# The head norm of a first attention block on Trainium2: totals, reciprocals and roots moved from 8-partition rows to token layout

## The chip, the cores and the metric

The kernel runs on one core of one Trainium2 chip. The metric is the device time of one execution in microseconds. The time of a kernel is the median of its runs.

## The reference

Two blocks of layers in sequence (the first with a differential and a neighbourhood attention, the second with a hybrid mixer and experts), in float32, over 512 tokens and 256 context tokens with a model width of 1024. The change lies in the first block's first attention, a differential attention with 8 heads of width 128:

```python
def _diff_attend(q, k, v, lam, subln, lam_init):
    s = jnp.einsum('bqhjd,bkhjd->bhjqk', q, k).astype(jnp.float32) * (HEAD_DIM ** -0.5)
    p = jax.nn.softmax(s, axis=-1)
    a = (p[:, :, 0] - lam * p[:, :, 1]).astype(v.dtype)
    o = jnp.einsum('bhqk,bkhe->bqhe', a, v)
    o = rmsnorm(o, subln) * (1.0 - lam_init)
    return o.reshape(o.shape[0], o.shape[1], -1)
```

So each of the 768 tokens has, for each of the 8 heads, a root mean square over the head's 128 features, by which the head's output is divided. The result is multiplied by `wo` and added to the residual stream.

## The kernel before, in words

The program is a sequence of stages; each is one block in which the five engines run their own instruction lists, written out by hand, and wait for each other by semaphores. No scheduler reorders anything. Activations are kept with features on the 128 partitions and tokens along the free dimension, so the attention output `o` is a tile of 128 partitions x 8 heads x 768 tokens: one head per chunk of 768 columns. `differential` (from L1539) fills it, and also leaves `rs`, the sums of the exponentials, with tokens on the partitions: 128 x 6 token tiles x 8 heads. It doesn't divide by those sums; the norm's small term `eps` is scaled by their square instead.

`residual` (L1147) is the stage that follows. It multiplies the normed `o` by `wo` in fp32 split into a rounded high part and a low part. For this first attention it has a `Heads` object (L1071), the head norm, whose steps stand ahead of the product:

- `squares` (ACT, L1087): for each head, the squares of its 768 columns into one of two buffers. The third and later squares wait until the totals of the head two before have been taken (`summed`).
- `tensor` (PE): first six transposes (L1100) turn `rs` into rows, 8 partitions x 768 tokens. Then for each head n the totals over the 128 partitions (L1105): the weights are 8 columns of the constant `pick`, of which only column n is ones, the 768 squares stream, and the result accumulates in PSUM into row n of 8. Then five products that nobody reads (L1109, `HEADS_IDLE`). Then, when the roots have come, the spreads.
- `vector` (DVE): copies the turned sums (L1127), squares them times eps (L1129), adds the totals (L1132), takes the reciprocal (L1134), waits for ACT's root, rounds it (L1136, `root_hi`, in the order's rows `lo_4389`) and takes the low part (L276, `root_lo`, `lo_4390`). All of these are 8 partitions x 768.
- `roots` (ACT, L1091): the square root. In ACT's list it stands behind the rounding of two weight chunks (L791), and its first use loads ACT's table.
- `spread` (PE, L1119 and L1120): copies one row of the roots to all 128 partitions. There are two PSUM places: `res_acc`'s last slot and `res_totals`. Spread c waits from c = 2 on for the scaling of head c - 2.
- `scale` (DVE, L1143), `high` (ACT, L1095) and the low part (DVE, L276): one head's output is scaled, rounded and split.
- `ring.multiply` (L270, L271, L824 and later L263 to L265): the first two of the eight output chunks are computed head by head as these become ready, with the spread of head c + 2 ahead of the products of head c. The other six follow, densely.

Elsewhere the kernel has sums of squares in another form: `Squares.tensor` (L506) loads the 128x128 squares of a token tile as weights and streams one column of ones, so that the total comes out with tokens on the partitions. `unread_products` (L460) issues products of the identity with constants that nobody reads. The same helper's lines are used in several stages.

Of the kernel before, what the change touches and what calls it, by code (L numbers as in the profile page):

```python
# [20 lines left out]
ACT = mybir.ActivationFunctionType  # L21
F32 = mybir.dt.float32
# [5 lines left out]
P = 128  # L28
D = 1024
KD = D // P  # L30
# [155 lines left out]
class Core:  # L186
# [5 lines left out]
    def __init__(self, nc):  # L192
        self.nc, self.n, self.fresh, self.spent, self.place = nc, 0, [], [], {}
        self.n_zeroing = 2 * (NE + NOVER)
# [79 lines left out]
def lo_of(engine, lo, value, hi):  # L274

    return engine.tensor_tensor(lo, value, hi.bitcast(F32), ALU.subtract)  # L276
# [180 lines left out]
def unread_products(K, bank, count):  # L457

    for _ in range(count):
        K.nc.tensor.matmul(bank, K.const("ident"), K.consts[:, 0:bank.shape[1]], start=True, stop=True)  # L460


class Squares:
# [37 lines left out]
    def tensor(self, pe):  # L501
        nc, one = self.K.nc, self.K.const("ones")[:, 0:1]

        def total(at, tile, tokens):
            for t in range(tokens // P):
                last = nc.tensor.matmul(self.totals[:, at + t:at + t + 1], tile[:, t * P:(t + 1) * P], one, start=True, stop=True)  # L506
            return last

        final = self.room[(KD - 1) % 2]
        pe.wait_ge(self.summed, KD - 2)  # L510
        last = total(0, self.sums, self.tok + self.extra)
        if self.weight is not None:
            last = total(NT, self.weighed, self.tok)
        last.then_inc(self.early, 1)
        if self.idle is not None:
            unread_products(self.K, self.totals[:, 640:896], 2)
        pe.wait_ge(self.squared, KD)
        last = total(512, final[0], self.tok)
        if self.weight is not None:
            last = total(512 + NT, final[1], self.tok)  # L520
        last.then_inc(self.late, 1)
        if self.idle is not None:
            unread_products(self.K, self.idle, 1)

    def vector(self, dve):
        nc, totals, ms, inv = self.K.nc, self.totals, self.ms, self.inv
        n, own = (self.tok + self.extra) // P, self.tok // P
        dve.wait_ge(self.early, 1)
        nc.vector.tensor_scalar(ms[:, 0:n], totals[:, 0:n], 1.0 / D, EPS, ALU.mult, ALU.add)
        if self.weight is not None:  # L530
            nc.vector.tensor_scalar(ms[:, NT:], totals[:, NT:NT + NTX], 1.0 / D, None, ALU.mult)
        dve.drain()
        dve.wait_ge(self.late, 1)
        nc.vector.scalar_tensor_tensor(ms[:, 0:own], totals[:, 512:512 + own], 1.0 / D, ms[:, 0:own], ALU.mult, ALU.add)
        if self.weight is not None:
            nc.vector.scalar_tensor_tensor(ms[:, NT:], totals[:, 512 + NT:512 + NT + NTX], 1.0 / D, ms[:, NT:], ALU.mult, ALU.add)
        dve.drain()
        last = nc.vector.reciprocal(inv[:, 0:n], ms[:, 0:n])
        if self.weight is not None:
            dve.drain()  # L540
            nc.vector.tensor_tensor(ms[:, NT:], ms[:, NT:], inv[:, 0:NTX], ALU.mult)
            dve.drain()
            nc.vector.tensor_scalar(ms[:, NT:], ms[:, NT:], EPS, None, ALU.add)
            dve.drain()
            last = nc.vector.reciprocal(inv[:, NT:], ms[:, NT:])
        last.then_inc(self.inverted, 1)
        if self.weight is not None:
            roots = self.K.roots
            dve.wait_ge(self.rooted, 1)
            nc.vector.tensor_tensor(roots[:, NT + NTX:], roots[:, 0:NTX], roots[:, NT:NT + NTX], ALU.mult)  # L550
            dve.drain()
# [207 lines left out]


ACCS = 3
HEADS_IDLE = 5


class Ring:
# [305 lines left out]
class Heads:  # L1071


    def __init__(self, K, ctx, src, tok, sums, eps, gain, room, totals, spreads, idle):
        self.K, self.src, self.tok, self.sums, self.eps, self.gain = K, src, tok, sums, eps, gain
        self.room, self.totals, self.spreads, self.idle = room, totals, spreads, idle
        self.rstd, self.floor = (K.sb(ctx, "heads_" + n, [KD, tok]) for n in ("rstd", "floor"))
        self.root_hi, self.root_lo = K.lo(self.floor), K.lo(self.rstd)
        self.rows = K.sb(ctx, "heads_rows", [KD, KD], FR)
        self.floor_full, self.squared, self.summed, self.inverted, self.rooted, self.split, self.spread_full, self.scaled, self.rounded = (  # L1080
            K.sem("heads_" + n) for n in ("floor", "squared", "summed", "inverted", "rooted", "split", "spread", "scaled", "hi"))

    def squares(self, act):
        for n in range(KD):
# [3 lines left out]

    def roots(self, act):
        act.wait_ge(self.inverted, 1)  # L1090
        self.K.nc.scalar.activation(self.rstd[:], self.rstd[:], ACT.Sqrt).then_inc(self.rooted, 1)  # L1091

    def high(self, act, hi, c):
        act.wait_ge(self.scaled, c + 1)
        self.K.nc.scalar.copy(hi[:, c, :], self.src[:, c, 0:self.tok]).then_inc(self.rounded, 1)  # L1095

    def tensor(self, pe, parts):
        nc, pick, ident = self.K.nc, self.K.const("pick"), self.K.const("ident")
        for t in range(self.tok // P):
            last = nc.tensor.transpose(self.spreads[0][0:KD, t * P:(t + 1) * P], self.sums[:, t, :], ident)  # L1100
        last.then_inc(self.floor_full, 1)
        for n in range(KD):
            pe.wait_ge(self.squared, n + 1)
            for a, b in parts:
                last = nc.tensor.matmul(self.totals[0:KD, a:b], pick[:, KD - 1 - n:2 * KD - 1 - n], self.room[n % 2][0][:, a:b],  # L1105
                                        start=(n == 0), stop=(n == KD - 1))
            last.then_inc(self.summed, 1)
        for _ in range(HEADS_IDLE):
            nc.tensor.matmul(self.idle, ident, self.K.consts[:, 0:512], start=True, stop=True)  # L1109
        pe.wait_ge(self.split, 1)  # L1110
        for c in range(2):
            self.spread(pe, c, parts)
# [8 lines left out]
        last.then_inc(self.spread_full, 1)  # L1121

    def vector(self, dve):
        nc, tok, rstd, floor = self.K.nc, self.tok, self.rstd, self.floor
        nc.vector.tensor_copy(self.rows[:], self.K.const("ident")[0:KD, 0:KD])
        dve.wait_ge(self.floor_full, 1)
        nc.vector.tensor_copy(rstd[:], self.spreads[0][0:KD, 0:tok])  # L1127
        dve.drain()
        nc.vector.scalar_tensor_tensor(floor[:], rstd[:], self.eps, rstd[:], ALU.mult, ALU.mult)  # L1129
        dve.drain()  # L1130
        dve.wait_ge(self.summed, KD)
        nc.vector.scalar_tensor_tensor(rstd[:], self.totals[0:KD, 0:tok], 1.0 / P, floor[:], ALU.mult, ALU.add)  # L1132
        dve.drain()
        nc.vector.reciprocal(rstd[:], rstd[:]).then_inc(self.inverted, 1)  # L1134
        dve.wait_ge(self.rooted, 1)
        nc.vector.tensor_copy(self.root_hi[:], rstd[:])  # L1136
        dve.drain()
        lo_of(nc.vector, self.root_lo[:], rstd[:], self.root_hi[:]).then_inc(self.split, 1)

    def scale(self, dve, c):  # L1140
        mine = self.src[:, c, 0:self.tok]
# [2933 lines left out]
```

## Time and profile before

| | us |
|---|---|
| median of 3 runs | 3480.74 |
| the runs | 3481.81, 3480.74, 3475.3 |
| the profiled execution | 3483.02 |
| its span | 3481.2 |
| PE busy | 3284.4 |
| DVE busy | 2272.3 |
| ACT busy | 1477.7 |
| POOL busy | 340.8 |

The median is of executions without a profile. The span is from the first to the last instruction of the profiled one; what is beyond it up to 3483.02 us lies before and after. The page shows by slices of 87 us how busy each engine is, and the clock that TensorE was granted, which has two levels, 2.4 GHz (1.00) and 1.2 GHz (0.50). PE is the engine for matmuls and PEld its weight loads, DVE is VectorE, ACT is ScalarE, POOL is GpSimd and SP is SyncE. One fp32 matmul shows as two records. Times in the trace are counted from the start of the span. The changed stage takes less than 30 us of it, so the slices are too coarse for it, and the trace is read by stretches and by instructions.

### The profile page before, as it was taken

How to read it: one execution, taken by the hardware profiler on the slowest of the kernel's cores; microseconds unless marked ns; L12 is line 12 of the kernel's file. 1: busy time of each engine (PE TensorE's matmuls, PEld its weight loads, DVE VectorE, ACT ScalarE, POOL GpSimd, SP SyncE). 2: the span in 40 equal slices, each digit the busy share in tenths (PEclk: the TensorE clock that was granted, in tenths of full speed). 3: DMA queues.
4: the chain of work that ended last, by engine and by line, in shares of the span. 5: the costliest groups of instructions: out<-in, count | busy, mean ns of one | idle time of the engine just before them, and what ended most of it. 6: DMA issues, size and time to landing. Idle time of an engine off the chain costs nothing. (4 is left out here: it accounts for less than half of the span.)

```text
span 3481.2 us, 46855 instructions
## 1 busy us (share of the span) xinstructions
PE 3284.4 (94%) x18748; PEld 2682.1 (77%) x18748; DVE 2272.3 (65%) x2962; ACT 1477.7 (42%) x1957; POOL 340.8 (10%) x217
## 2 busy tenths in 40 slices
PE   7998999999999999999999998899889989999996
PEld 5886778888888896778888778779677766777774
DVE  6467746756666227758776555665765358888885
ACT  5216633212123117733233443443433247777774
POOL 0020000000000000000000013321200013222221
PEclk9999999999999999999999999999999999999998
DMA  6540013354533221045654239111023259999993
GB/s 246 197 167 13 1 49 109 115 175 134 177 109 100 71 72 44 22 131 189 225 182 130 74 92 273 30 37 49 25 61 85 61 207 380 384 369 366 380 359 114
DMA packets 371666, 522.63 MB, mean 150 GB/s; under 512 B 19618, under 2 KB 313122, under 8 KB 345872
## 3 DMA queue, kind: packets, MB, share of 16 engines
q1 hardware_dynamic: 362112, 503.25, 43.1%
q0 software_dynamic: 9360, 16.72, 1.4%
q8 instruction: 129, 2.11, 0.2%
q14 instruction: 65, 0.53, 0.0%
HBM read 484.46 MB, written 51.90 MB: 154 GB/s over the span
## 5 line engine op out<-in xcount | busy, mean ns | idle before, releaser
L276 DVE TENSOR_TENSOR lo<-exp_raw,exp_hi 128x2048 fp32r<-128x2048 f32 x192 | 439.0, 2290 | 65.1 <-ACT exp_hi L3651 65.1
L3651 ACT CAST exp_hi<-exp_raw 128x2048 fp32r<-128x2048 f32 x192 | 366.5, 1913 | 113.4 <-PE exp_down_acc L265 49.6
L264 PE MATMUL ffn_acc<-lo,up_w_hi 128*128 128x512 f32 x1140 | 406.7, 357 | 0.0
L263 PE MATMUL ffn_acc<-normed_hi,up_w_hi 128*128 128x512 f32 x1008 | 360.0, 357 | 11.0 <-DVE lo L276 11.0
L444 DVE SCALAR_TENSOR_TENSOR aside_w<-aside_w,aside_c 128x1024 f32<-128x1024 f32 x176 | 213.0, 1233 | 81.2 <-DMA aside_w<-in_ada_t 73.0
L264 PEld LDWEIGHTS ffn_acc<-lo,up_w_hi 128*128 128x128 f32 x1140 | 216.0, 189 | 33.5
L263 PEld LDWEIGHTS ffn_acc<-normed_hi,up_w_hi 128*128 128x128 f32 x1008 | 190.8, 189 | 41.7 <-DVE lo L276 12.6
L1418 ACT ACTIVATE conv<-ffn_acc,vecs 128x768 f32<-128x768 f32 (+1 forms) x88 | 73.1, 881 | 297.7 <-PE ffn_acc L265 297.7
L265 PE MATMUL ffn_acc<-normed_hi,lo 128*128 128x512 f32 (+1 forms) x528 | 190.0, 360 | 0.0
L265 PE MATMUL ffn_acc<-gated_hi,lo 128*128 128x512 f32 (+1 forms) x528 | 187.9, 356 | 0.0
L265 PE MATMUL ffn_acc<-normed_hi,up_w_lo 128*128 128x512 f32 x480 | 170.4, 355 | 0.0
L1483 DVE SCALAR_TENSOR_TENSOR conv<-ffn_acc,vecs,conv 128x511 f32<-128x511 f32 (+1 forms) x132 | 79.1, 655 | 125.0 <-ACT conv L1418 125.0
L263 PE MATMUL ffn_acc<-gated_hi,down_w_hi 128*128 128x512 f32 (+1 forms) x396 | 142.1, 359 | 3.6 <-DVE lo L276 3.6
L264 PE MATMUL ffn_acc<-lo,down_w_hi 128*128 128x512 f32 (+1 forms) x396 | 142.2, 359 | 0.0
L265 PE MATMUL feat_acc<-normed_hi,lo 128*128 128x512 f32 (+1 forms) x400 | 139.0, 348 | 0.0
L263 PE MATMUL feat_acc<-normed_hi,lo 128*128 128x512 f32 x368 | 127.3, 346 | 1.6 <-DVEq L728 1.6
L264 PE MATMUL feat_acc<-lo,lo 128*128 128x512 f32 x368 | 127.6, 347 | 0.0
L263 PE MATMUL tok_acc<-tok_w_hi,normed_hi 128*128 128x256 f32 x384 | 114.2, 297 | 3.0 <-DVEq L1039 1.7
L276 POOL TENSOR_TENSOR lo<-res_w,res_w_hi 128x1024 fp32r<-128x1024 f32 x4 | 9.6, 2419 | 1062.2 <-ACT res_w_hi L685 1062.2
L265 PEld LDWEIGHTS ffn_acc<-normed_hi,lo 128*128 128x128 f32 x528 | 100.4, 190 | 15.0
L265 PEld LDWEIGHTS ffn_acc<-gated_hi,lo 128*128 128x128 f32 x528 | 100.1, 190 | 15.0
L264 PE MATMUL tok_acc<-lo,normed_hi 128*128 128x256 f32 x384 | 107.3, 279 | 0.0
(677 smaller groups left out, 8920.6 us busy)
## 6 DMA issues: line engine op xcount, KB each, us to landing
exp_raw<-in_w_experts SPq DMA_DIRECT2D x192, 1024.0 KB, 8.2
aside_w<-in_ada_t SPq DMA_DIRECT2D x176, 512.0 KB, 6.3
up_w<-in_ffn_up SPq DMA_DIRECT2D x88, 512.0 KB, 5.2
x_rows<-dn_zero SPq DMA_DIRECT2D x42, 384.0 KB, 5.3
y_rows<-dn_zero SPq DMA_DIRECT2D x42, 384.0 KB, 5.3
ada_w<-in_ada_first SPq DMA_DIRECT2D x8, 1024.0 KB, 13.0
v<-in_ada_t SPq DMA_DIRECT2D x16, 512.0 KB, 6.7
gate_w<-in_w_in SPq DMA_DIRECT2D x16, 512.0 KB, 5.3
```

The costliest lines, as they stand in the source:

```text
L263: nc.tensor.matmul(out, left[0], right[0], start=start, stop=False)
L264: nc.tensor.matmul(out, left[0], right[1], start=False, stop=False)
L265: return nc.tensor.matmul(out, left[1], right[0], start=False, stop=stop)
L276: return engine.tensor_tensor(lo, value, hi.bitcast(F32), ALU.subtract)
L444: self.K.nc.vector.scalar_tensor_tensor(tile[:], tile[:], 1.0, self.cond[layer // 2, s][:], ALU.mult, ALU.mult, accum_out=self.K.mods[:, l ...
L1418: last = nc.scalar.activation(conv[:, u, s, :], acc[:, u, s, 0:tok], ACT.Identity, bias=K.vecs[:, at(n + (b0 + n0 + s * NF))], scale=K.vec ...
L1483: nc.vector.scalar_tensor_tensor(conv[:, u, s, a + 1:b], acc[:, u, s, a:b - 1], K.vecs[:, at(n + (tap0 + n0 + s * NF))], conv[:, u, s, a + ...
L3651: nc.scalar.copy(hi[slot(e, j)][:], raw[tile(e, j)][:]).then_inc(tile_hi[j], 1)
```

## The change

Everything up to the roots stays with tokens on the partitions. The totals are taken with the squares of a token tile as weights and one column of ones streaming, 48 products in all (8 heads x 6 tiles), each with its own column of PSUM. The sums `rs` are used as they lie. DVE's square, addition and reciprocal, and ACT's root, work on 128 partitions x 48. PE then turns the roots into 8 rows x 768 by six transposes; DVE rounds and splits them straight from PSUM. The five unread products become one behind the totals and one behind the transposes.

```diff
@@ -759,7 +759,6 @@
 
 
 ACCS = 3
-HEADS_IDLE = 5
 
 
 class Ring:
@@ -1077,8 +1076,9 @@
         self.rstd, self.floor = (K.sb(ctx, "heads_" + n, [KD, tok]) for n in ("rstd", "floor"))
         self.root_hi, self.root_lo = K.lo(self.floor), K.lo(self.rstd)
         self.rows = K.sb(ctx, "heads_rows", [KD, KD], FR)
-        self.floor_full, self.squared, self.summed, self.inverted, self.rooted, self.split, self.spread_full, self.scaled, self.rounded = (
-            K.sem("heads_" + n) for n in ("floor", "squared", "summed", "inverted", "rooted", "split", "spread", "scaled", "hi"))
+        self.floors, self.inverse, self.turnable = (K.sb(ctx, "heads_" + n, [P, tok // P, KD]) for n in ("floors", "inverse", "roots"))
+        self.turned, self.squared, self.summed, self.inverted, self.rooted, self.split, self.spread_full, self.scaled, self.rounded = (
+            K.sem("heads_" + n) for n in ("turned", "squared", "summed", "inverted", "rooted", "split", "spread", "scaled", "hi"))
 
     def squares(self, act):
         for n in range(KD):
@@ -1088,25 +1088,27 @@
 
     def roots(self, act):
         act.wait_ge(self.inverted, 1)
-        self.K.nc.scalar.activation(self.rstd[:], self.rstd[:], ACT.Sqrt).then_inc(self.rooted, 1)
+        self.K.nc.scalar.activation(self.turnable[:], self.inverse[:], ACT.Sqrt).then_inc(self.rooted, 1)
 
     def high(self, act, hi, c):
         act.wait_ge(self.scaled, c + 1)
         self.K.nc.scalar.copy(hi[:, c, :], self.src[:, c, 0:self.tok]).then_inc(self.rounded, 1)
 
     def tensor(self, pe, parts):
-        nc, pick, ident = self.K.nc, self.K.const("pick"), self.K.const("ident")
-        for t in range(self.tok // P):
-            last = nc.tensor.transpose(self.spreads[0][0:KD, t * P:(t + 1) * P], self.sums[:, t, :], ident)
-        last.then_inc(self.floor_full, 1)
+        nc, one, ident = self.K.nc, self.K.const("ones")[:, 0:1], self.K.const("ident")
+        tiles = self.tok // P
         for n in range(KD):
             pe.wait_ge(self.squared, n + 1)
-            for a, b in parts:
-                last = nc.tensor.matmul(self.totals[0:KD, a:b], pick[:, KD - 1 - n:2 * KD - 1 - n], self.room[n % 2][0][:, a:b],
-                                        start=(n == 0), stop=(n == KD - 1))
+            for t in range(tiles):
+                last = nc.tensor.matmul(self.totals[:, t * KD + n:t * KD + n + 1], self.room[n % 2][0][:, t * P:(t + 1) * P], one,
+                                        start=True, stop=True)
             last.then_inc(self.summed, 1)
-        for _ in range(HEADS_IDLE):
-            nc.tensor.matmul(self.idle, ident, self.K.consts[:, 0:512], start=True, stop=True)
+        unread_products(self.K, self.idle, 1)
+        pe.wait_ge(self.rooted, 1)
+        for t in range(tiles):
+            last = nc.tensor.transpose(self.spreads[0][0:KD, t * P:(t + 1) * P], self.turnable[:, t, :], ident)
+        last.then_inc(self.turned, 1)
+        unread_products(self.K, self.idle, 1)
         pe.wait_ge(self.split, 1)
         for c in range(2):
             self.spread(pe, c, parts)
@@ -1121,21 +1123,20 @@
         last.then_inc(self.spread_full, 1)
 
     def vector(self, dve):
-        nc, tok, rstd, floor = self.K.nc, self.tok, self.rstd, self.floor
+        nc, tok = self.K.nc, self.tok
         nc.vector.tensor_copy(self.rows[:], self.K.const("ident")[0:KD, 0:KD])
-        dve.wait_ge(self.floor_full, 1)
-        nc.vector.tensor_copy(rstd[:], self.spreads[0][0:KD, 0:tok])
-        dve.drain()
-        nc.vector.scalar_tensor_tensor(floor[:], rstd[:], self.eps, rstd[:], ALU.mult, ALU.mult)
+        nc.vector.scalar_tensor_tensor(self.floors[:], self.sums, self.eps, self.sums, ALU.mult, ALU.mult)
         dve.drain()
         dve.wait_ge(self.summed, KD)
-        nc.vector.scalar_tensor_tensor(rstd[:], self.totals[0:KD, 0:tok], 1.0 / P, floor[:], ALU.mult, ALU.add)
+        nc.vector.scalar_tensor_tensor(self.floors[:], self.totals[:, 0:tok // P * KD].rearrange("p (t n) -> p t n", n=KD), 1.0 / P,
+                                       self.floors[:], ALU.mult, ALU.add)
         dve.drain()
-        nc.vector.reciprocal(rstd[:], rstd[:]).then_inc(self.inverted, 1)
-        dve.wait_ge(self.rooted, 1)
-        nc.vector.tensor_copy(self.root_hi[:], rstd[:])
+        nc.vector.reciprocal(self.inverse[:], self.floors[:]).then_inc(self.inverted, 1)
+        dve.wait_ge(self.turned, 1)
+        turned = self.spreads[0][0:KD, 0:tok]
+        nc.vector.tensor_copy(self.root_hi[:], turned)
         dve.drain()
-        lo_of(nc.vector, self.root_lo[:], rstd[:], self.root_hi[:]).then_inc(self.split, 1)
+        nc.vector.tensor_tensor(self.root_lo[:], turned, self.root_hi[:].bitcast(F32), ALU.subtract).then_inc(self.split, 1)
 
     def scale(self, dve, c):
         mine = self.src[:, c, 0:self.tok]
```

On PE, in the stage of the head norm, from its start to the first spread. Names: `square_216` and `square_217` are the two buffers, `rs` the sums, `res_acc` and `res_totals` PSUM. Before:

```order
L1100 MATMUL res_acc<-consts,rs 8x128 x6
L1105 MATMUL res_totals<-square_216,consts 8x512
L1105 MATMUL res_totals<-square_216,consts 8x256
L1105 MATMUL res_totals<-square_217,consts 8x512
L1105 MATMUL res_totals<-square_217,consts 8x256
...
L1109 MATMUL res_acc<-consts 128x512 x5
L1119 MATMUL res_acc<-lo_4389,heads_rows 128x512
L1120 MATMUL res_acc<-lo_4390,heads_rows 128x512
```

And now:

```order
L1103 MATMUL res_totals<-consts,square_216 128x1 x6
L1103 MATMUL res_totals<-consts,square_217 128x1 x6
...
L460 MATMUL res_acc<-consts 128x512
L1109 MATMUL res_acc<-consts,heads_roots 8x128 x6
L460 MATMUL res_acc<-consts 128x512
L1121 MATMUL res_acc<-lo_4389,heads_rows 128x512
L1122 MATMUL res_acc<-lo_4390,heads_rows 128x512
```

The sixteen streaming products (of 512 and 256 columns) became eight groups of six products of one column; the transposes moved from ahead of them to behind them; three of the five unread products are gone.

On DVE, in the same place. Before:

```order
L1125 CAST heads_rows<-consts 8x8
L1127 COPY heads_rstd<-res_acc 8x768
L1129 SCALAR_TENSOR_TENSOR heads_floor<-heads_rstd 8x768
L1132 SCALAR_TENSOR_TENSOR heads_rstd<-res_totals,heads_floor 8x768
L1134 RECIPROCAL heads_rstd<-heads_rstd 8x768
L1136 CAST lo_4389<-heads_rstd 8x768
L276 TENSOR_TENSOR lo_4390<-heads_rstd,lo_4389 8x768
L1143 SCALAR_TENSOR_TENSOR o<-o,subln,res_acc 128x768
```

And now:

```order
L1127 CAST heads_rows<-consts 8x8
L1128 SCALAR_TENSOR_TENSOR heads_floors<-rs 128x48
L1131 SCALAR_TENSOR_TENSOR heads_floors<-res_totals,heads_floors 128x48
L1134 RECIPROCAL heads_inverse<-heads_floors 128x48
L1137 CAST lo_4389<-res_acc 8x768
L1139 TENSOR_TENSOR lo_4390<-res_acc,lo_4389 8x768
L1144 SCALAR_TENSOR_TENSOR o<-o,subln,res_acc 128x768
```

One copy is gone, three operations shrank from 8 x 768 to 128 x 48, and the last two now read PSUM.

## Rows read from the trace of the kernel before

**Rows 1.** The page, part 1: busy time, share of span, instructions.

```profile
PE 3284.4 (94%) x18748; PEld 2682.1 (77%) x18748; DVE 2272.3 (65%) x2962; ACT 1477.7 (42%) x1957; POOL 340.8 (10%) x217
```

**Rows 2.** Stretches: length, busy us (instructions) per engine, granted clock, DMA share, GB/s.

```profile
432.00:434.00 2.00, 1.12 (x8) 0.69 (x7) 0.00 (x0) 0.75 (x3) 0.00 (x0) 1.00 0.00 0
...
450.20:454.20 4.00, 0.01 (x1) 0.00 (x0) 3.02 (x3) 0.84 (x1) 0.00 (x0) 0.76 0.00 0
454.20:462.30 8.10, 8.05 (x23) 6.59 (x24) 4.69 (x5) 2.50 (x3) 0.00 (x0) 0.50 0.01 2
462.30:482.50 20.20, 20.20 (x106) 16.12 (x105) 12.72 (x14) 4.18 (x5) 0.00 (x0) 1.00 0.00 0
```

**Rows 3.** Timeline of the head norm: start, length, engine, line [idle before, releaser].

```profile
434.36 0.82 PE L1100 MATMUL res_acc<-consts,rs 128*8 128x128 f32 x6 [0.61 <-PEq L250]
435.24 10.49 PE L1105 MATMUL res_totals<-square,consts 128*8 128x512 f32 x32
438.02 0.84 ACT L1087 ACTIVATE square<-o 128x768 f32<-128x768 f32 x1 [0.45 <-PE res_totals L1105]
443.93 1.98 ACT L791 CAST lo<-v 128x1024 fp32r<-128x1024 f32 x2
445.65 4.56 PE L1109 MATMUL res_acc<-consts 128*128 128x512 f32 x10
445.76 0.95 DVE L1132 SCALAR_TENSOR_TENSOR heads_rstd<-res_totals,heads_floor 8x768 f32<-8x768 f32 x1 [8.57 <-PE res_totals L1105]
445.92 1.28 ACT L1091 ACT_TABLE_LOAD   x1
446.78 4.94 DVE L1134 RECIPROCAL heads_rstd<-heads_rstd 8x768 f32<-8x768 f32 x1
451.76 0.84 ACT L1091 ACTIVATE heads_rstd<-heads_rstd 8x768 f32<-8x768 f32 x1 [4.55 <-DVE heads_rstd L1134]
452.63 0.55 DVE L1136 CAST lo<-heads_rstd 8x768 fp32r<-8x768 f32 x1 [0.91 <-ACT heads_rstd L1091]
453.25 0.95 DVE L276 TENSOR_TENSOR lo<-heads_rstd,lo 8x768 fp32r<-8x768 f32 x1
454.25 0.79 PE L1119 MATMUL res_acc<-lo,heads_rows 8*128 8x512 f32 x1 [4.04 <-DVE lo L276]
```

**Rows 4.** Timeline, PE: first product of the third, fourth and fifth spread.

```profile
457.00 0.79 PE L1119 MATMUL res_acc<-lo,heads_rows 8*128 8x512 f32 x1
...
462.64 0.49 PE L1119 MATMUL res_totals<-lo,heads_rows 8*128 8x512 f32 x1
...
465.80 0.50 PE L1119 MATMUL res_acc<-lo,heads_rows 8*128 8x512 f32 x1
```

**Rows 5.** Timeline, PE, end of the same stage: one-column totals at clock 1.00.

```profile
532.48 1.40 PE L506 MATMUL res_totals<-consts,square_sums 128*128 128x1 f32 x12
533.74 1.11 PE L460 MATMUL res_totals<-consts 128*128 128x256 f32 x4
```

**Rows 6.** Timeline, PE, start of the program: one-column totals.

```profile
14.12 2.72 PE L506 MATMUL ada_totals<-consts,square_sums 128*128 128x1 f32 x12 [14.12 <-DMA rows<-in_rows]
16.71 2.70 PE L506 MATMUL ada_totals<-consts,square 128*128 128x1 f32 x12
```

**Rows 7.** Stretches at the end of the second feed-forward stage.

```profile
1909.70:1913.10 3.40, 3.40 (x29) 3.30 (x28) 0.56 (x5) 2.52 (x3) 0.00 (x0) 1.00 0.00 0
1913.10:1916.50 3.40, 3.10 (x9) 1.56 (x9) 1.27 (x9) 0.21 (x1) 0.00 (x0) 0.51 0.00 0
```

**Rows 8.** Timeline, PE, there.

```profile
1908.78 1.39 PE L506 MATMUL ffn_acc<-consts,square_sums 128*128 128x1 f32 x12
1910.03 1.03 PE L506 MATMUL ffn_acc<-consts,weighed_sums 128*128 128x1 f32 x8
1910.93 1.11 PE L460 MATMUL ffn_acc<-consts 128*128 128x256 f32 x4
1911.87 2.25 PE L506 MATMUL ffn_acc<-consts,conv 128*128 128x1 f32 x16
```

**Rows 9.** Lines L538 and L556: durations in ns, min/median/max.

```profile
L538 DVE RECIPROCAL inverse<-mean_squares x6: 178/192/193, 19.7 to 2821.0; 128x6 f32<-128x6 f32 x4, 128x4 f32<-128x4 f32 x2
...
L556 ACT ACTIVATE roots<-inverse x6: 205/208/212, 22.3 to 2821.2; 128x6 f32<-128x6 f32 x3, 128x4 f32<-128x4 f32 x2, 128x10 f32<-128x10 f32 x1
```

## The prediction

> **What bounds the kernel now.** I read the page's first table first: PE is busy for 3284.4 us, 94% of the span [rows 1]. A change to a small stage therefore counts by what it does to the stretches in which PE waits and by the speed at which PE runs. The chain that ended last shows only the end of the program, so I read the stage itself: first by stretches [rows 2], then in order of time [rows 3]. The head norm begins at 434.3 us and ends, for this question, where the first matmul of the spread starts, at 454.25. What the reader should see in it:
>
> - 435.24 to 445.7: the eight totals. PE is busy without a gap. The 32 records take 10.49 us, 1.3 a head, of which ACT's square is 0.84; before each square ACT waits 0.45 for PE (six such rows). PE sets this pace.
> - 445.76 to 454.25: a serial chain of 8.5 us. DVE adds the floor (0.95), takes reciprocals on 8 partitions x 768 (4.94), ACT takes roots (0.84), DVE rounds (0.55) and takes the low part (0.95). PE fills the first 4.5 us with unread products and then idles for 4.0.
> - After that idle stretch the granted clock is 0.50 for 8.1 us and returns to 1.00 at about 462.3 [rows 2].
>
> The price of the low clock in the part that follows: one head's spread and products take 3.16 us at full clock (462.64 to 465.80), while those that began at 457.00 took 5.64 [rows 4]. Had the clock been full from 454.25 on, the third spread after the first (462.64) would have come at about 459.6: spread 0.9, scaling 1.0, rounding 0.85 and products 2.3 (3.16 less the spread) in sequence, with 0.3 of hops. So the low clock costs 3.0 us there.
>
> **The totals.** The number of PE cycles doesn't change. Before, 8 columns of `pick` are the weights and 768 squares stream past. Now the squares are the weights, in six loads of 128x128, and one column of ones streams. The stage that sums squares at 532.48 shows this form: six products, twelve records, take 1.26 us from start to start of what follows [rows 5]. Eight heads are 10.1 to 10.3 us, against 10.5. So at full clock the totals gain 0.2 to 0.4 us, no more. The six transposes of the sums and two DVE passes that vanish from the start were hidden behind ACT's first square and the totals: nothing.
>
> **The clock during the totals** is the term that decides. The same products ran at the start of the program for over 5 us in one piece, twelve records in 2.59 us and twice as long as the 1.26 above, so at 1.2 GHz, and the second twelve were no faster than the first [rows 6]. And from 1909.70 to 1913.10 PE shows 3.40 us busy of 3.40 at clock 1.00, and the next stretch is at 0.51 [rows 7]. What PE did before that fall was almost nothing but such one-column products: 36 records from 1908.78 on, with one pair of unread products between them [rows 8]. The fall came 4.3 us after their start. In the changed kernel they run for over 10 us with nothing else in between. I therefore take the clock to fall to 1.2 GHz within the totals. The Trainium skill says otherwise: TensorE: Matmul & The Clock Gate, Part 1, has the clock gate follow how busy PE has been and warns of idle gaps; by it a queue without gaps stays at full clock, and the sum would end at -7.1 us (the rival below). By that rule, the trace disagrees: PE was busy for all 3.40 us ahead of the fall [rows 7].
>
> When does it fall? Between 435.2 (at once) and 440 (4.3 us in, and a little more). In the case at 1909 PE came from dense products; here it comes from the thin end of the attention, busy for 1.12 us of 2 [rows 2]. I take 437. Then 1.4 heads run at 1.28 us and 6.6 at 2.56 (twelve records at the start of the program took 2.59 [rows 6]): 1.8 + 16.9, so the totals end at 453.9 instead of 445.7. With the bounds: 455.7 and 451.0.
>
> **From the last total to the first spread.** Now the arithmetic is 128 x 48. Adding the floor: 0.2 us, as the smallest DVE operations. Reciprocal: 0.19 us for six columns [rows 9] and 4.94 for 768 [rows 3] give 6.2 ns a column, so 0.45. With the gaps of the engine, inverted after 0.75. Root: 0.26 (0.21 for six columns [rows 9]). The loading of ACT's table takes 1.28 us and stands behind two roundings of 1.98 [rows 3]; at the slow pace the last square ends 4.3 us before the totals do, so both are over in time and cost nothing. Without that cover, at full clock, they end 3.3 us after the last square, 1.65 after the last total, and hold the root back by 0.9. Next PE: the one unread product behind the totals takes 0.9 us at full clock (five in 4.56 us [rows 3]) and 1.8 at half, so PE is ready at 1.8, after the root. Here the change adds a wait: PE stands for ACT's root, and behind it in PE's list are the transposes and all spreads, for which DVE and ACT's eight roundings wait. Six transposes: 0.82 us at full clock [rows 3], 1.5 at half: 3.3. DVE then rounds and subtracts straight from PSUM. The trace has no such rounding; the nearest rows are 0.55 for the rounding from SBUF and 0.95 for an operation of the same size that reads PSUM (445.76), and I take the latter, since the source is what changes: 0.95 + 0.07 + 0.95. The second unread product runs beside it. Sum 5.4 us, against 8.5 before. So the first spread starts at 459.3, not 454.25: **+5.05 us** (bounds +2.2 and +6.9, from the fall at 440 and at 435.2).
>
> **The clock after it.** Before, the low clock lasted 8 us beyond the first spread and cost 3.0. Now PE has been at work on two unread products, the transposes and the spreads from 453.9 on, with short waits, so it should come back sooner; 8.1 us after the work began, as here with its waits, would be 462, and it can be sooner. What can be won is between 0 and 3.0; I take 1.2, below the middle, since the waits stay between.
>
> Sum: +5.05 - 1.2 = **+3.9 us**. The profiled execution took 3483.02 us for its span of 3481.2, so 3486.9; it stood 2.3 us above the median of 3480.74, which gives **3484.6**. The bounds are -0.8 and +6.9, with the runs shown spread over 6.5 us besides.
>
> Nothing else moves. The DMA loads of the stage land at its start. All of this is small: about 0.2%, or 7 us, is what a measurement of this kernel can tell from no change.
>
> **Rivals.**
> - *Slower: the clock falls at once and stays low through two more heads.* For it: the attention's end is thin and the six transposes that ran at 434.36 are gone [rows 3]; low stretches after waits lasted 8 us already. Against it: two unread products. Price: totals to 455.7, spread at 461.1 (+6.9), and the low clock up to two us longer than before beyond the spread, +1 to +2: about +8.5, 3489. It decides if the fall comes before 436 and the return after 464. 0.18.
> - *Faster: the clock holds.* Totals end at 445.4; the root waits for ACT's table; spread 4.8 us later, at 450.2, -4.05; with no 4 us of idleness the clock stays up and the 3.0 are won too: -7.1, 3473.7. Against it stand [rows 6] and [rows 7]; for it, only that PE has no gap. 0.12.
> - *The clock holds in the totals and falls after them*, as before: only -4, 3476.7. 0.04.
> - *The chain is not much shorter*, if DVE's three operations on 128x48 cost nearer the 0.95 of the old form than 0.2 to 0.45: about 2 us more, 3486.7. The 0.19 us for six columns speaks against it. 0.02.
>
> **How the numbers follow.** My forecast has 0.64: between -0.8 and +6.9, with the likeliest value at 3484.6. The range of 3477 to 3491 takes in its bounds, the slow rival and some of the spread between runs; what is left out is the clock that holds and part of the tails. Faster by over 0.2% (below 3473.8): half of the clock that holds, 0.07 with a stray run. Slower by over 0.2% (above 3487.7): most of the slow rival and the upper end of the forecast, 0.22. Within: 0.71.
>
> **What would show it.** In the profile of the changed kernel: a granted clock of 0.50 before 440 and through most of the totals; the 96 one-column records, twelve in about 2.6 us; DVE's 128x48 reciprocal under 0.6 us; the table load finished before the reciprocal ends; the first spread near 459; full clock again by 463. If instead twelve of them take 1.3 us throughout, the deciding step is wrong and the kernel is faster by about 7 us. If the first spread comes near 459 but the time is unchanged, the return of the clock was worth the full 3 us.

## The result, and the profile after

Over 22 runs of each, the changed kernel takes 3485.78 us (median) against 3479.71 us: a ratio of 1.0015, with a 95% interval of 1.001 to 1.0021. It is slower by 6.1 us between the medians, or by 5 us as the ratio has it (0.15% of 3480): clear of noise, and inside the 0.2% that the prediction named as its bound. The forecast was 3484.6 us; it expected +3.9 us, and +6.1 came.

The profiled execution took 3490.07 us, the slowest of its 22, so its trace shows an expensive case. The page:

```profile
span 3488.1 us, 46969 instructions
PE 3293.1 (94%) x18806; PEld 2696.3 (77%) x18806; DVE 2264.9 (65%) x2961; ACT 1477.5 (42%) x1957; POOL 339.7 (10%) x217
```

The stage by stretches, the changed kernel (columns as in [rows 2]): the last 2 us before and in the first totals, the totals, the chain to the first spread, the head-by-head part; three pieces around the clock's return at 459.6, its fall at 463.0 and its next return at 480.1 (0.50 in between); and all that follows.

```profile
434.30:436.30 2.00, 0.82 (x5) 0.82 (x5) 0.27 (x2) 1.58 (x2) 0.00 (x0) 0.85 0.22 46
...
435.48:455.90 20.42, 20.42 (x97) 20.42 (x97) 0.00 (x0) 8.90 (x10) 0.00 (x0) 0.51 0.20 52
455.90:461.18 5.28, 4.39 (x12) 1.66 (x11) 2.55 (x4) 0.24 (x1) 0.00 (x0) 0.65 0.00 0
461.18:493.90 32.72, 32.31 (x128) 25.58 (x129) 17.45 (x19) 6.67 (x8) 0.00 (x0) 0.74 0.00 1
...
459.60:463.00 3.40, 2.34 (x10) 1.26 (x8) 2.27 (x3) 0.00 (x0) 0.00 (x0) 1.00 0.00 0
463.00:466.40 3.40, 3.15 (x9) 2.53 (x10) 3.40 (x5) 2.06 (x3) 0.00 (x0) 0.50 0.00 0
...
480.10:484.00 3.90, 3.90 (x20) 2.96 (x19) 1.88 (x2) 0.83 (x1) 0.00 (x0) 1.00 0.00 0
...
493.90:3488.10 2994.20, 2842.91 (x16022) 2321.36 (x16020) 1956.64 (x2478) 1265.11 (x1539) 308.83 (x195) 0.98 0.47 156
```

In the kernel before, the same three pieces of the stage are:

```profile
435.24:445.70 10.46, 10.46 (x33) 2.81 (x33) 1.87 (x2) 7.41 (x9) 0.00 (x0) 1.00 0.37 100
445.70:454.25 8.55, 4.51 (x11) 1.77 (x10) 7.38 (x4) 2.33 (x3) 0.00 (x0) 0.88 0.00 0
454.25:482.57 28.32, 28.32 (x129) 22.77 (x129) 17.48 (x19) 6.67 (x8) 0.00 (x0) 0.85 0.00 1
...
482.57:3481.20 2998.63, 2847.74 (x16022) 2327.08 (x16020) 1958.13 (x2478) 1265.04 (x1539) 309.40 (x195) 0.98 0.47 156
```

The totals grew from 10.5 us to 20.4, the chain shrank from 8.55 to 5.28, and the head-by-head part grew from 28.3 to 32.7. The stage ends 11.3 us later (493.90 against 482.57). The rest of the program, whose code is the same, happened to be 4.4 us shorter in this execution (2994.2 against 2998.6).

In order of time, the changed kernel, to be held against [rows 3]:

```profile
435.48 20.45 PE L1103 MATMUL res_totals<-consts,square 128*128 128x1 f32 x96 [1.48 <-ACT square L1087]
...
450.84 0.84 ACT L1087 ACTIVATE square<-o 128x768 f32<-128x768 f32 x1 [1.72 <-PE res_totals L1103]
...
453.58 1.28 ACT L1091 ACT_TABLE_LOAD   x1
455.79 2.06 PE L460 MATMUL res_acc<-consts 128*128 128x512 f32 x2
455.96 0.21 DVE L1131 SCALAR_TENSOR_TENSOR heads_floors<-res_totals,heads_floors 128x48 f32<-128x48 f32 x1 [21.09 <-PE res_totals L1103]
456.24 0.45 DVE L1134 RECIPROCAL heads_inverse<-heads_floors 128x48 f32<-128x48 f32 x1
456.73 0.24 ACT L1091 ACTIVATE heads_roots<-heads_inverse 128x48 f32<-128x48 f32 x1 [1.86 <-DVE heads_inverse L1134]
457.63 1.49 PE L1109 MATMUL res_acc<-consts,heads_roots 128*8 128x128 f32 x6
459.16 0.95 DVE L1137 CAST lo<-res_acc 8x768 fp32r<-8x768 f32 x1 [2.46 <-PE res_acc L1109]
460.18 0.94 DVE L1139 TENSOR_TENSOR lo<-res_acc,lo 8x768 fp32r<-8x768 f32 x1
461.18 0.49 PE L1121 MATMUL res_acc<-lo,heads_rows 8*128 8x512 f32 x1 [0.89 <-DVE lo L1139]
```

The reader should see three things. PE has no gap in the totals, and the clock is 0.50 all the same; ACT's idle time before each square rose from 0.45 to 1.72 us because it waits for PE. The reciprocal fell from 4.94 us to 0.45 and the root from 0.84 to 0.24. And the table load is over at 454.86 (453.58 and 1.28), before the reciprocal begins at 456.24, so the root never waits for it.

### The profile page after: what moved, and what is told of

Its sections match the earlier page's. It is cut to its first block and busy times, and to the rows that moved or that the text cites. A ratio compares the mean times of both kernels' runs of the same rounds, so it can differ in the third digit from the quotient of the medians.

```text
span 3488.1 us, 46969 instructions
## 1 busy us (share of the span) xinstructions
PE 3293.1 (94%) x18806; PEld 2696.3 (77%) x18806; DVE 2264.9 (65%) x2961; ACT 1477.5 (42%) x1957; POOL 339.7 (10%) x217
## 5 line engine op out<-in xcount | busy, mean ns | idle before, releaser
L263 PE MATMUL ffn_acc<-normed_hi,up_w_hi 128*128 128x512 f32 x1008 | 360.2, 357 | 10.8 <-DVE lo L276 10.8
L263 PEld LDWEIGHTS ffn_acc<-normed_hi,up_w_hi 128*128 128x128 f32 x1008 | 190.7, 189 | 41.9 <-DVE lo L276 12.4
L263 PE MATMUL ffn_acc<-gated_hi,down_w_hi 128*128 128x512 f32 (+1 forms) x396 | 140.9, 356 | 3.0 <-DVE lo L276 3.0
L263 PE MATMUL feat_acc<-normed_hi,lo 128*128 128x512 f32 x368 | 127.1, 345 | 1.6 <-DVEq L728 1.6
L263 PE MATMUL tok_acc<-tok_w_hi,normed_hi 128*128 128x256 f32 x384 | 114.7, 299 | 3.2 <-DVEq L1038 1.7
L265 PE MATMUL tok_acc<-tok_w_hi,lo 128*128 128x256 f32 x384 | 108.1, 281 | 0.0
```

Source lines behind the costliest of these rows:

```text
L263: nc.tensor.matmul(out, left[0], right[0], start=start, stop=False)
L265: return nc.tensor.matmul(out, left[1], right[0], start=False, stop=stop)
```

## The experiments

All of them concern this one stage. For each trace I read two lengths: from ACT's first square to the first spread, and from there to the first product of the dense part (L263). The ratio is against the kernel before, run on the same chip at the same time. Where the text gives us for a ratio, they are its share of 3480 us; the medians themselves give somewhat other values (e5 -2.0, e7 -8.4, e8 -14.3).

| kernel | to the first spread | to the dense part | ratio (95%) |
|---|---|---|---|
| before, two traces | 19.91, 19.91 | 28.3, 30.4 | 1 |
| changed, three traces | 26.6, 26.8, 26.8 | 32.7, 27.9, 27.9 | 1.0015 (1.001 to 1.0021) |
| e1, 128 columns in the totals | 17.9 | 26.8 | 0.9983 (0.9975 to 0.9992) |
| e2, changed with spreads of 128 partitions | 26.5 | 23.3 | 1.0006 (0.9997 to 1.0015) |
| e3, before with nine unread products | 19.9 | 25.2 | 0.9997 (0.9988 to 1.0006) |
| e4, row totals, arithmetic in token layout | 18.6 | 26.7 | 0.9982 (0.9973 to 0.999) |
| e5, e1 with the root earlier | 17.4 | 26.7 | 0.999 (0.998 to 1.0) |
| e6, e5 with spreads of 128 partitions | 17.5 | 23.3 | 0.9984 (0.9975 to 0.9993) |
| e7, e6 with an unread product at the start | 15.9 | 23.3 | 0.9974 (0.9962 to 0.9985) |
| e8, e4 with both | 17.1 | 23.3 | 0.9962 (0.9949 to 0.9976) |
| e9, before with spreads of 128 partitions | 19.9 | 24.3 | 0.9982 (0.9973 to 0.9991) |

One trace can't rank two of these kernels by its whole length. Behind the stage all of them run the same code, and that code took from 2989.5 us (e8) to 3004.1 us (e7) in these traces, a wider spread than any effect in the table. So the stage is read from the traces, and the time from the medians and ratios.

**e1: the same weight loads, more columns.** The totals' `one` becomes 128 columns of ones; the column of PSUM follows the order of issue, so that later products overwrite what isn't needed.

```diff
-                last = nc.tensor.matmul(self.totals[:, t * KD + n:t * KD + n + 1], self.room[n % 2][0][:, t * P:(t + 1) * P], one,
+                at = n * tiles + t
+                last = nc.tensor.matmul(self.totals[:, at:at + P], self.room[n % 2][0][:, t * P:(t + 1) * P], ones,
```

> The changed kernel, but each of the 48 totals streams 128 columns of ones instead of one; the further columns are overwritten or never read. Same weight loads, same number of products. Theory (the one-column products let the clock fall): the granted clock stays at 1.00 through the totals, a group of twelve records takes 1.3 to 1.45 us, the totals end near 446.5 instead of 455.8, the first spread comes at 451 to 452. Against the kernel before: -2 to -6 us, depending on whether the clock falls later in the short waits. Rival (the fall comes from the thin end of the attention, or from the waits at the stage's start, whatever the products are): the clock falls near 436 as before, a group takes 2.6 us or more, and the time is +6 us or worse.

```profile
434.50:437.80 3.30, 3.03 (x14) 3.03 (x15) 0.00 (x0) 1.01 (x3) 0.00 (x0) 0.50 0.89 248
437.80:447.00 9.20, 9.20 (x84) 9.20 (x84) 0.00 (x0) 6.62 (x8) 0.00 (x0) 1.00 0.11 27
447.00:451.75 4.75, 2.72 (x12) 0.96 (x11) 2.55 (x4) 1.79 (x3) 0.00 (x0) 1.00 0.00 0
451.75:478.51 26.76, 26.35 (x128) 21.20 (x129) 17.44 (x19) 6.68 (x8) 0.00 (x0) 0.94 0.00 1
```

This decides between the two explanations. PE was busy without a gap in both forms; only the number of streamed columns differs, and here the clock rose to 1.00 within the totals at 437.8 and stayed there, where with one column it stayed at 0.50 to the end. The first 3.3 us are low here too, which the expectation had not allowed for, so the start of the stage has a low stretch of its own (see e7). e5, e6 and e7 stream 128 columns as well, and in each of their traces the clock is at 1.00 for the last 9 us of the totals or more. The kernel is 0.17% faster than before, as expected, and 0.32% faster than the changed one by the two ratios.

**e2: spreads that read 128 partitions.** `rstd`, `floor` and `rows` get 128 partitions; DVE clears the first two at the start, and the roots still fill eight of them.

```diff
-        row = self.rows[:, c:c + 1].broadcast_to([KD, P])
+        row = self.rows[:, c:c + 1].broadcast_to([P, P])
...
+        zeros = self.K.x[:, 0, 0:tok]
+        nc.vector.tensor_tensor(self.root_hi[:], zeros, zeros, ALU.subtract)
+        nc.vector.tensor_tensor(self.root_lo[:], zeros, zeros, ALU.subtract)
```

> The changed kernel, but the spreads read all 128 partitions (zeros beyond the eight rows of roots) instead of 8; columns and count are the same, so PE's time for them at a given clock is the same. Theory (spreads from eight partitions don't bring the clock back, which is why it stayed low for 17 us beside a PE that had no gap): the totals still run at the low clock to about 455.8 and the first spread comes at about 461, but the clock is at 1.00 for good by 468 instead of 480.1, and the time is +2 to +4 us against before instead of +6. Rival (the number of partitions doesn't matter, the long low stretch comes from the waits): low until about 480 again, +6 us.

```profile
436.11:456.30 20.19, 20.19 (x96) 20.19 (x97) 1.14 (x4) 8.90 (x10) 0.00 (x0) 0.51 0.20 53
456.30:461.72 5.42, 4.62 (x12) 1.80 (x12) 2.55 (x4) 0.24 (x1) 0.00 (x0) 0.63 0.00 0
461.72:484.99 23.27, 22.86 (x128) 19.78 (x129) 17.44 (x19) 6.68 (x8) 0.00 (x0) 1.00 0.00 1
```

The totals are as low and as long as in the changed kernel, the second trace of one-column totals that shows this. The head-by-head part went from 27.9 or 32.7 us to 23.3 at clock 1.00. The measured 1.0006, some 3 us less than the changed kernel's, agrees with the expected +2 to +4 against before, though its interval reaches to no change and overlaps the changed kernel's.

**e3: PE's gap filled in the kernel before.** `HEADS_IDLE = 9` in place of 5.

> The kernel before, with nine unread products behind the totals instead of five, which fill PE's 4.0 us of idle time (5 products took 4.56 us, so 9 take some 7.8 of the 8.5). Theory (the low clock after that gap costs 3.0 us): clock 1.00 from 450 to 463 in most executions, -2 to -3 us against before. Rival (the clock falls in the part after the first spread anyway, because of its own waits): 0 to -1 us.

```profile
433.58:444.00 10.42, 10.42 (x32) 2.77 (x33) 1.88 (x2) 7.37 (x9) 0.00 (x0) 1.00 0.36 101
444.00:452.60 8.60, 7.99 (x19) 3.34 (x19) 7.38 (x4) 2.38 (x3) 0.00 (x0) 1.00 0.00 0
452.60:477.79 25.19, 24.78 (x129) 19.93 (x129) 17.45 (x19) 6.68 (x8) 0.00 (x0) 1.00 0.00 1
```

In the trace the clock never falls, and the head-by-head part takes 25.2 us instead of 28.3: the low clock had cost 3.1, where the prediction had 3.0. Yet the ratio is 0.9997 with 1 in its interval, so against -2 to -3 us expected the time shows -1 and can't be told from no change. The mechanism is seen in the trace; that it is worth anything in the median is not shown.

**e4: half of the change.** The totals go back to the form before, into rows; DVE copies them out, six transposes turn them, and the 128 x 48 arithmetic and the way back stay as changed.

```diff
+        nc.vector.tensor_copy(self.rstd[:], self.totals[0:KD, 0:tok]).then_inc(self.kept, 1)
...
+        pe.wait_ge(self.kept, 1)
+        for t in range(tiles):
+            at = BACK + t * KD
+            last = nc.tensor.transpose(self.spreads[0][:, at:at + KD], self.rstd[:, t * P:(t + 1) * P], ident[0:KD, 0:KD])
+        last.then_inc(self.back, 1)
```

> Half of the change alone: the totals as in the kernel before (768 columns stream past 8 columns of weights, result in eight rows), then copied out of PSUM and turned to token layout by six transposes; floor, reciprocal and root on 128 x 48 and the way back as in the changed kernel. Theory (the arithmetic in token layout is a gain, the loss is the clock in the totals): clock 1.00 through the totals, which end at 445.7; the first spread about 6.3 us later, at 452.0 against 454.25 before; -1 to -4 us against before. Rival (the shorter chain is eaten by the added copy, transposes and hops): the first spread at 454 or later, no gain.

```profile
435.40 12.18 PE L1105 MATMUL res_totals<-square,consts 128*8 128x512 f32 x32 [1.48 <-ACT square L1089]
...
448.62 0.53 PE L1112 MATMUL res_acc<-consts,heads_rstd 8*128 8x8 f32 x6
...
450.25 0.82 PE L1117 MATMUL res_acc<-consts,heads_roots 128*8 128x128 f32 x6
```

The chain after the totals takes 5.5 us, where 6.3 was expected. The totals took 12.2 us and not 10.5, because this form too has the low stretch at the start (the clock was 0.50 from 436.2 to 439.7), which I had not expected. Even so: 0.9982. The arithmetic in token layout is a gain; with either other form of totals, e1's or this one, the kernel is faster than before, and only with the one-column form is it slower.

**e5: the root ahead of ACT's weight roundings.** In ACT's list `heads.roots` moves before the two `ring.high`, and a second unread product follows the transposes.

> The kernel of e1 (128 columns stream in the totals), with ACT's root ahead of the rounding of two weight chunks, so that its table is loaded during the last totals, and a second unread product behind the transposes. Theory (the root waited for the table: 448.58 to 448.8 in e1, 0.7 us after the reciprocal): root 1.05 us after the last total, first spread 3.9 us after it instead of 4.5 to 4.7; -0.6 us against e1, and a little more where the added unread product keeps the clock: about -6.5 us against before. Rival (the roundings of the weights, now later, hold up the first rounding of a head): -5 us or less, with ACT busy with weights when the first head is scaled.

The first spread comes 4.0 us after the last total's end (447.0 to 450.98) instead of e1's 4.6, about as expected, and the trace's stage is 0.6 us shorter than e1's. The rival's cause isn't seen: ACT is done with the weights at 449.92 and then idle for 3.1 us before the first head's rounding. The time is 0.999, -3.5 us instead of -6.5, and the intervals of e1 and e5 overlap: a step of half a microsecond is below what these runs can tell.

**e6: e5 with the spreads of e2.**

> The kernel of e5 with spreads that read 128 partitions, as in e2. Theory (products from eight partitions don't hold the clock; that is why in e1 it fell at 454.9 for 3.4 us): clock 1.00 from the totals to the end of the head-by-head part in most executions, -7 to -9 us against before. Rival (the short waits between the spreads let it fall): as e5, -6 us.

The head-by-head part takes 23.3 us at clock 1.00, and the time is 0.9984, or -5.6 us; expected were -7 to -9.

**e7: e6 with one unread product at the start.**

```diff
+        unread_products(self.K, self.idle, 1)
         for n in range(KD):
             pe.wait_ge(self.squared, n + 1)
```

> The kernel of e6 with one more unread product at the start of the stage, in the 0.9 us in which PE waits for ACT's first square. Theory (the low clock from 434.4 to 437.8 in e1, and from 436.2 to 439.7 in e4, comes from that wait together with the thin end of the attention): no low clock at the start of the totals, which then take 11.3 us instead of 12.3; -1 us against e6, -8 to -10 against before. Rival (one product of 0.9 us is too little): as e6.

```profile
433.37 1.10 PE L460 MATMUL res_acc<-consts 128*128 128x512 f32 x2 [0.61 <-PEq L250]
434.30 10.93 PE L1105 MATMUL res_totals<-consts,square 128*128 128x128 f32 x96
```

The totals take 10.9 us instead of 12.4 or 12.6, with no low clock at their start. The three kernels whose list at the start held the transposes (before, e3, e9) didn't have it either; the six without them and without this product (changed, e1, e2, e4, e5, e6) all had it. The six transposes that the change moved away from there seem to have done a job that no one had given them; no run puts them back alone, but the split is complete. 0.9974, -9 us, where -8 to -10 was expected; its interval overlaps e6's.

**e8: e4 with the spreads of e2 and the unread product at the start.**

> The kernel of e4 (row totals, arithmetic in token layout) with spreads from 128 partitions and the unread product at the start. Theory: totals 10.5 us at full clock, the chain after them 5.5 us, no low clock in the stage; the first spread at about 451.5; -8 to -10 us against before, within 1 us of e7, whose totals are 0.8 us longer and whose chain is 1.6 us shorter. Rival (the clock falls in the chain's waits all the same): as e4, -6 us.

```profile
433.20:444.70 11.50, 11.46 (x35) 3.09 (x35) 2.02 (x4) 8.28 (x10) 0.00 (x0) 1.00 0.34 91
444.70:450.30 5.60, 4.36 (x19) 1.76 (x19) 3.50 (x5) 1.76 (x3) 0.00 (x0) 1.00 0.00 0
450.30:473.57 23.27, 22.86 (x128) 19.80 (x129) 17.46 (x19) 6.69 (x8) 0.00 (x0) 1.00 0.00 1
```

Clock 1.00 in the whole stage, and the lowest ratio of all: 0.9962, -13 us, faster than both kernels, from five runs. That it beats e7 is not shown: the intervals overlap, and e7's stage is 1.2 us the shorter in the traces (39.1 against 40.3). The stage itself is 7.9 us shorter than in the first trace of before. The interval begins at 0.9976, -8.4 us, so the trace's saving lies just short of it. The rest lies behind the stage in this trace: the same code took 2989.5 us there against 2998.6, and the granted clock over the whole execution was 0.983 against 0.978. Whether the edit brings that about or the executions happened so is not settled, and I wouldn't count on more than the 8 or 9.

**The changed kernel and the one before again.**

> The changed kernel again, for a second trace. Theory (one-column totals always let the clock fall; how long it stays low after the spreads depends on where its changes happen to lie against the stage): the totals again at 0.50 from before 440 to about 455.8, the clock back at 1.00 at some time between 459 and 480, and the first product of the dense part (493.9 in the first trace, 482.6 in the kernel before) between 485 and 494. Rival (the 17 us of low clock are fixed by the kernel): low until 480 again, 493.9.

> The changed kernel a third time, with the same expectations as for the second: if the three traces differ in when the clock comes back, but not in the totals, the theory holds.

> The kernel before again. Theory: totals at clock 1.00; after the gap of PE's 4.0 us the clock falls in some executions and in others perhaps later, and comes back at different times, so the dense part starts between 479.5 and 486 (482.6 in the first trace).

These are single executions, taken for their traces: 3487.08 and 3488.32 us for the changed kernel, 3484.0 for the one before.

The changed kernel, second trace:

```profile
434.20:454.50 20.30, 20.26 (x95) 20.26 (x96) 0.00 (x0) 8.94 (x10) 0.00 (x0) 0.50 0.19 52
...
458.10:461.50 3.40, 2.26 (x9) 1.23 (x9) 2.26 (x3) 0.00 (x0) 0.00 (x0) 1.00 0.00 0
461.50:468.30 6.80, 6.54 (x20) 4.90 (x19) 4.30 (x5) 2.50 (x3) 0.00 (x0) 0.50 0.00 0
468.30:488.00 19.70, 19.70 (x104) 15.92 (x104) 12.73 (x14) 4.18 (x5) 0.00 (x0) 1.00 0.00 1
```

The totals are the same in all three traces; what differs is how long the clock stays low afterwards: 17 us in the first, 6.8 in the other two. In the kernel before it was 10.3 and, in the second trace, 13.6 (453.3 to 466.9), with the dense part at 484.5. The rival of a fixed 17 us falls.

**e9: only the spreads changed, in the kernel before.**

> The kernel before, with only the spreads changed: they read 128 partitions (zeros beyond the eight rows). Theory (beside the clock, the change of the weights' partitions costs PE 0.2 us on either side of each spread, 0.4 us a head: 3.17 us in the kernel with nine unread products against 2.77 in e2): the first spread at the same 19.9 us after the first square as before; from there to the dense part 23.3 to 25.5 us instead of 28.3, with the clock falling at most for a window's worth after PE's gap; -2.5 to -5 us against before, ratio 0.9986 to 0.9993. Rival (the gain in e2, e6, e7 and e8 came from their other edits): 28 us again, ratio 1.000.

```profile
444.40:453.01 8.61, 4.57 (x12) 1.82 (x11) 7.38 (x4) 2.39 (x3) 0.00 (x0) 1.00 0.00 0
453.01:477.35 24.34, 24.07 (x129) 20.79 (x130) 17.46 (x19) 6.69 (x8) 0.00 (x0) 0.93 0.00 1
```

24.3 us, within the 23.3 to 25.5 expected, and 0.9982, slightly more of a gain than expected. The clock did fall after PE's 4 us gap, at 454.4, but was back by 457.8. The gain of the full spreads stands on its own.

## Why the prediction was right, and where it was off

- **"The number of PE cycles doesn't change."** Right as far as the runs show: no trace has the one-column totals at full clock, but their 20.45 us at half clock would be 10.2 at full, against 10.49 before. e7, with 128 columns at full clock, takes 10.9.
- **"The clock during the totals."** Right, and the deciding step. It was at 0.50 in all four traces with one-column totals, beside a busy PE. The rule that a queue without gaps holds the clock, from the Trainium skill (TensorE: Matmul & The Clock Gate, Part 1), would have given -7. By that rule, the traces disagree: e1 and the changed kernel differ in the totals only in the columns, PE shows no gap in either, and the clock is 1.00 in one from 437.8 on and 0.50 in the other to the end.
- **"When does it fall?"** This is the first mis-sized term. I took 437, between 435.2 and 440; in the first trace it came at 435.7, 0.2 us behind the first total's start, and in the two others at 434.2 and 434.3, just before it. I had the thin end of the attention in view, but costed the removed transposes at nothing; e7 shows that PE's idle 0.9 us in their place is part of the cause. So the totals took all of the 20.4 us, and the first spread came 6.7 to 6.9 us later than before instead of 5.05: the upper bound that I had worked out.
- **"From the last total to the first spread," 5.4 us.** 5.39 (455.79 to 461.18), with the parts as priced: 0.21 and 0.45 on DVE (0.2, 0.45), 0.24 for the root (0.26), 1.49 for the transposes (1.5), 0.95 and 0.94 from PSUM (0.95 each), the table load hidden. At full clock, too: I had 4.8 with the wait for the table, and e1 has 4.7.
- **"The clock after it," -1.2 us.** The second mis-sized term, and the wrong step in kind. The clock did come back early, at 459.6, before the first spread; then it fell again at 463.0, after a wait for DVE and two spreads. From the first spread to the dense part the three traces take 32.7, 27.9 and 27.9 us, 29.5 on average, and the two of before 28.3 and 30.4, 29.3. The credit was nothing. 5.05 and -1.2 became 6.8 and 0.2, a sum of 7 from few traces, where the median says 6.1. Both errors point the same way. That the time still fell within 1.2 us of the forecast is in part luck: the sum was 2.2 us short, but it stood on 3480.74 us for the kernel before, and the median of all its runs is 3479.71.
- **The slower rival**, which I gave 0.18, is what the traces show: it was to decide if the clock fell before 436 and returned after 464. It fell before 436 in all three, and came back for good at 480.1 in the first and at 468 in the other two (with 3.4 us of full clock in between, which it did not foresee). Its price of +8.5 was too high for the median, which is between it and the forecast.
- **The faster rivals** are out: the totals ran at half clock each time. So is the chain that is not much shorter: DVE's three operations on 128x48 took 0.19, 0.21 and 0.45 us.
- **A misread row.** I counted six rows in which ACT waits 0.45 for PE before a square. There are five; the sixth wait, the first of them, is 0.81. Nothing in the sum hangs on it.

## What to carry to other kernels

Moving an arithmetic chain from 8 partitions to 128 shortens it as its rows say (here 8.5 us to 5.3), but the form of the products that go with it has to be judged as well, not for their cycles but for the clock that they leave behind: here 20 us of one-column products ran at 1.2 GHz in all four traces, however busy PE looked. If such a form is wanted for its layout, let it stream more columns, whose results may be overwritten (128 were enough here), or keep the old form and turn its result. And before costing a removed instruction at nothing, look at what the engine's clock does around it: the six transposes here were priced at nothing, and only where they stood, or an unread product in their place, were the totals free of a low stretch of 3.4 us at the start.

## What the runs showed that I had not expected

**The partitions of the weights cost PE time.** In the head-by-head part at clock 1.00 throughout, 25.2 us with spreads from 8 partitions (e3) became 23.3 with 128 (e2, e6, e7, e8), although the columns and their number are the same. e3, one spread and what follows it (PEld is the weight load):

```profile
466.57 0.85 PE L824 MATMUL res_acc<-lo,res_w_hi 128*128 128x512 f32 x4
467.36 0.18 PEld L1119 LDWEIGHTS res_acc<-lo,heads_rows 8*128 8x128 f32 x1 [0.24 <-issue]
467.36 0.49 PE L1119 MATMUL res_acc<-lo,heads_rows 8*128 8x512 f32 x1
...
468.24 0.19 PEld L270 LDWEIGHTS res_acc<-res_hi,res_w_hi 128*128 128x128 f32 x1
```

e2, the same place:

```profile
466.15 0.85 PE L823 MATMUL res_acc<-lo,res_w_hi 128*128 128x512 f32 x4
466.73 0.19 PEld L1121 LDWEIGHTS res_totals<-lo,heads_rows 128*128 128x128 f32 x1
466.85 0.40 PE L1121 MATMUL res_totals<-lo,heads_rows 128*128 128x512 f32 x1
...
467.43 0.19 PEld L270 LDWEIGHTS res_acc<-res_hi,res_w_hi 128*128 128x128 f32 x1
467.54 0.39 PE L270 MATMUL res_acc<-res_hi,res_w_hi 128*128 128x512 f32 x1
```

With 128 partitions the weight load starts ahead of its product (466.73 for 466.85) while the one before runs. With 8 it starts only together with it, after 0.24 us of idle weight loading, and after the switch back the load again starts only with its product: from the last product group's start to the spread's, 0.79 us against 0.70, and from the spread's start to the next group's, 0.88 against 0.69. That is 0.28 us; the first product behind the switch back, 0.50 us against 0.39, adds 0.1. From spread to spread it is 3.16 to 3.20 us in e3 and 2.77 to 2.80 in e2, e7 and e8. The clean pair is before and e9, which differ in the spreads alone: 3.16 us at full clock before (462.64 to 465.80 in [rows 4]), and in e9:

```profile
464.77 0.40 PE L1120 MATMUL res_totals<-lo,heads_rows 128*128 128x512 f32 x1
...
467.57 0.39 PE L1120 MATMUL res_acc<-lo,heads_rows 128*128 128x512 f32 x1
```

**The 8-partition spreads may also not hold the clock.** It fell in the head-by-head part of every trace of the changed kernel and of e1, e4 and e5, and in none of e2, e6, e7 and e8. In e3, whose spreads have 8 partitions, it didn't fall. In the kernel before it fell within PE's 4 us gap and stayed low for 10.3 and 13.6 us, and with full spreads (e9) it was low for 3.4. No run separates the partitions from the shorter waits that come with them, so this stays open.
